# Causal mask added by TensorE: a matmul with the identity, one minimum over both groups, exponential from PSUM

## The chip, the core and the metric

The kernel runs on one core of a Trainium2 chip (trn2). The metric is the device time of one execution in microseconds (us).

## What is computed

One inference step of a two-layer decoder for a prompt of 512 tokens and 8 short sample sequences. Layer 0 is retention with spatial gating, layer 1 is native sparse attention (NSA), and each has a gated MLP behind it. The change touches only the prompt's share of the attention in layer 1. There are 16 query heads in 4 groups of 4, with a head width of 64, and three branches, each with its own keys and values:

```python
# compressed: 31 blocks of keys, masked by block end, softmax, times v
# selected (br 0) and window (br 1), with SEQ = 512: WINDOW = 512, and SEL_TOPK = 16 >= 8 blocks,
# so both are plain causal attention over all keys
s = jnp.einsum('bqgrd,bkgd->bqgrk', q, k).astype(jnp.float32) * ATTN_SCALE
s = jnp.where(mask, s, NEG)
p = jax.nn.softmax(s, axis=-1)
o = jnp.einsum('bqgrk,bkgd->bqgrd', p, v)
...
o = gates[0] * o_c + gates[1] * o_s + gates[2] * o_w
```

## The kernel before

Each engine has one program, written in its own block, and its instructions run in the order in which they stand there. Semaphores join the engines; `order(ins, sem)` counts a semaphore up when the instruction is done.

The stage runs over 72 units. `attention_unit(n)` splits n into a pair of groups j (0 or 1), a query tile qt of 128 queries (0 to 3), and w from 0 to 8. With w = 0 it is the compressed branch for all four heads of both groups; with w > 0 it is one head r and one branch br, for both groups of the pair at once. A unit with w > 0 has keys = (qt + 1) * 128 keys, that is one to four key tiles, so nine units in a row (a "group" of units) have the same length, and the lengths one to four come twice.

For a unit with w > 0 the work is:

- PE, `scores(n)`: one fp32 matmul per group g2 into its own half of `gemm[n % 2]`, two PSUM banks. The contraction is over 64 rows.
- DVE, `mask(n)`: for each g2 one `tensor_tensor_reduce`: scores times -SCALE plus a causal mask, into SBUF `pr[:, n % 4]`, with the minimum over the keys in `negmax`. The mask tile `causal` has 128 x 512 numbers, zero or 1e30 with a negative sign, of which the last `keys` columns are read.
- ACT, `exps(n)`: for each g2 the exponential in place in `pr`, with scale -1, bias `negmax` and the row sum in `rsum`.
- DVE, `normalise(n)`, one unit later: the reciprocal of the sums. POOL: `pr` times reciprocal times gate.
- PE, `turn_probs(n)`, three units later (LAG = 3): transposes of `pr` into `misc`, one per key tile and g2. Then ACT (n even) or DVE (n odd), `take_probs(n)`: copy of `misc` into `pT`.
- PE, `mix_values(n)`, four units later: `pT` times v into the accumulator of the group; after its nine units ACT and DVE take the heads into hH and hL.

The order on PE is scores(n), turn_probs(n - 3), mix_values(n - 4). On DVE it is mask(n), normalise(n - 1), take_probs(n - 3); on ACT exps(n), take_probs(n - 3). The queries and keys themselves are transposed on PE before and at the start of the stage (`turn_in`) and copied to `qTs`, `ksT`, `kwT` by ACT and DVE in turn (`take_in`). `scores(n)` reuses the bank pair of unit n - 2. The masks are loaded on POOL's queue under the semaphore `b_in`.

The helper `activate` records every ACT instruction at line 1142, and `turn` every transpose at line 552. The scores are lines 973 and 978, the products with v 1003 and 1009, the masks 1777 to 1786.

Of the kernel before, what the change touches and what calls it, by code (L numbers as in the profile page):

```python
# [33 lines left out]
ALU = mybir.AluOpType  # L34
ACT = mybir.ActivationFunctionType
AX_X = mybir.AxisListType.X

P = 128
D = 1024
DC = D // P  # L40
SEQ, DB, DS = 512, 8, 4
# [8 lines left out]
G, R, HD = 4, 4, 64  # L50
# [9 lines left out]
SCALE = HD ** -0.5  # L60
NEG = -1e30
BIG = 3e38
# [11 lines left out]
def shape_constants():  # L74

    pos = np.concatenate([np.tile(PAST + np.arange(DS), DB), np.arange(SEQ)]).astype(np.float64)
    ang = THETA_E[:, None] * pos[None, :]
    c = {}
    c["cos_even"] = np.concatenate([np.cos(ang), np.cos(ang)], 0)
    c["sin_even"] = np.concatenate([-np.sin(ang), np.sin(ang)], 0)  # L80
    co, so = np.zeros((P, NT, 8)), np.zeros((P, NT, 8))
    for t in range(NT):
        a = pos[tile_start(t):tile_start(t) + P, None] * THETA_O[None, :]
        co[:, t], so[:, t] = np.cos(a), np.sin(a)
    c["cos_odd"], c["sin_odd"] = co.reshape(P, -1), so.reshape(P, -1)
    i = np.arange(P)
    diff = i[None, :] - i[:, None]
    dm = np.zeros((P, RH, P))
    for h in range(RH):
        dm[:, h] = np.where(diff >= 0, GAMMA[h] ** np.maximum(diff, 0), 0)  # L90
    c["decay"] = dm.reshape(P, -1)
    s = np.arange(NS)
    ds = np.zeros((NS, RH, NS))
    same = (s[:, None] // DS) == (s[None, :] // DS)
    for h in range(RH):
        d = (s % DS)[None, :] - (s % DS)[:, None]
        ds[:, h] = np.where(same & (d >= 0), GAMMA[h] ** np.maximum(d, 0), 0)
    c["decay_s"] = ds.reshape(NS, -1)
    c["qdecay"] = np.stack([GAMMA[h] ** (i + 1.0) for h in range(RH)]).reshape(1, -1)
    c["qdecay_s"] = np.stack([GAMMA[h] ** (s % DS + 1.0) for h in range(RH)]).reshape(1, -1)  # L100
    c["kdecay"] = np.concatenate([np.stack([GAMMA[h] ** (P - 1.0 - i) for h in range(RH)], 1),
                                  np.stack([GAMMA[h] ** (DS - 1.0 - i % DS) for h in range(RH)], 1)], 1)
    c["tril_t"] = (diff >= 0).astype(np.float64)
    c["same_s"] = same.astype(np.float64)
    c["row_of_s"] = (np.arange(DS)[:, None] == (s % DS)[None, :]).astype(np.float64)
    c["batch_of"] = (s[:, None] // DS == np.arange(DB)[None, :]).astype(np.float64)
    c["ident"] = np.eye(P)
    sel = np.zeros((P, 4, P))
    for q in range(4):
        sel[32 * q, q] = 1  # L110
    c["spread"] = sel.reshape(P, -1)
    x = np.arange(SEQ)
    c["causal"] = np.where(x[None, :] - (SEQ - P) <= i[:, None], 0, NEG)
    cm, cv = np.zeros((P, 4, NCP)), np.zeros((P, 4, NCP))
    for t in range(4):
        ok = (np.arange(NCP) * 16 + 31)[None, :] <= (P * t + i)[:, None]
        cm[:, t], cv[:, t] = np.where(ok, 0, NEG), ok
    c["cmp_mask"], c["cmp_valid"] = cm.reshape(P, -1), cv.reshape(P, -1)
    n = i % 4
    new = np.full((P, DB, DB, DS), NEG)  # L120
    for b in range(DB):
        new[:, b, b, :] = np.where(np.arange(DS)[None, :] <= n[:, None], 0, NEG)
    c["mask_new"] = new.reshape(P, -1)
    pj = np.zeros((P, 2, NCS))
    for j in range(2):
        pj[:, j] = ((i // 64) == j)[:, None]
    c["pair_of"] = pj.reshape(P, -1)
    return {k: np.ascontiguousarray(v, dtype=np.float32) for k, v in c.items()}
# [51 lines left out]
def build_program(nc, a, o):  # L180
    with ExitStack() as ctx:
# [9 lines left out]
        def sb(name, shape, dt=F32, at=None):  # L191
            size = int(np.prod(shape[1:])) * 4
            size = (size + 31) // 32 * 32
            off = place["at"] if at is None else at
            assert off + size <= nc.sbuf_usable_end, (name, off, size)
            t = nc.alloc_sbuf_tensor_at(name, shape, dt, offset=off)
            if at is None:
                place["at"] = off + size
            return t
# [92 lines left out]
        place["at"] = O1  # L292
        qT1, ksT, kwT = sb("qT1", [P, R, SEQ]), sb("ksT", [P, 2, SEQ]), sb("kwT", [P, 2, SEQ])
        pr = sb("pr", [P, 4, 2, SEQ])
        causal = sb("causal_sb", [P, SEQ])
        cmask, cvalid = sb("cmask", [P, 4, NCP]), sb("cvalid", [P, 4, NCP])
        cmx, crs = sb("cmx", [P, 2, R]), sb("crs", [P, 3, 2, R])
        negmax, rsum, rscale = sb("negmax", [P, 4, 2]), sb("rsum", [P, 4, 2]), sb("rscale", [P, 4, 2])
# [133 lines left out]

        def masks_done(n):

            grp, w = n // 9, n % 9
            return 17 * grp + (2 * w + 1)

        def exps_done(n):

            grp, w = n // 9, n % 9  # L440
            return 16 * grp + 2 * w
# [106 lines left out]
        def _(pe):  # L548
# [410 lines left out]
            meet(pe, order, 3)  # L959


            def scores(n):

                j, qt, w, r, br = attention_unit(n)
                slot = gemm[n % 2]
                if n >= 2:
                    pe.wait_ge(masked, masks_done(n - 2))
                rows = slice(qt * P, (qt + 1) * P)
                if w == 0:
                    for r in range(R):  # L970
                        for g2 in range(2):
                            half = slice(64 * g2, 64 * g2 + 64)
                            ins = pe.matmul(slot[:, g2, r * NCP:(r + 1) * NCP], qTs[j][half, r, rows], kcP[half, j, :], start=True, stop=True)
                else:
                    keys = (qt + 1) * P
                    for g2 in range(2):
                        half = slice(64 * g2, 64 * g2 + 64)
                        ins = pe.matmul(slot[:, g2, 0:keys], qTs[j][half, r, rows], (ksT, kwT)[br][half, j, 0:keys], start=True, stop=True)  # L978
                order(ins, s_done)

            def turn_probs(n):
# [156 lines left out]
        def _(act):  # L1138
            order = Order(act, act_c)

            def activate(out, in_, func, sem_=None, **kw):
                order(act.activation(out, in_, func, **kw), sem_)  # L1142
# [229 lines left out]
            def exps(n):  # L1372
                _, qt, w, _, _ = attention_unit(n)
                if w == 0:
                    act.wait_ge(c_sub, n // 9 + 1)
                    part = pr[:, n % 4, :, 0:R * NCP]
                    activate(part, part, ACT.Exp, c_exped, scale=SCALE)
                    return
                keys = (qt + 1) * P
                for g2 in range(2):  # L1380
                    act.wait_ge(masked, masks_done(n) + g2 - 1)
                    part = pr[:, n % 4, g2, 0:keys]
                    activate(part, part, ACT.Exp, exped, bias=negmax[:, n % 4, g2:g2 + 1], scale=-1.0, accum_out=rsum[:, n % 4, g2:g2 + 1])

            def take_probs(n):

# [14 lines left out]
            def take_in(n):  # L1401
                j, z = TURNS[n]
                act.wait_ge(qk_turned, n + 1)
                activate(qTs[j][:, z, :] if z < R else (ksT, kwT)[z - R][:, j, :], misc[:, 2 + n % 2 if n < 6 else 3, :], ACT.Copy, qk_ev[0])

            act.wait_ge(gemm_done, FIRST_CHUNK[O_OUT])
            for n in range(0, 6, 2):
# [68 lines left out]
        def _(dve):  # L1476
# [293 lines left out]
            def mask(n):  # L1770
                _, qt, w, _, _ = attention_unit(n)
                dve.wait_ge(s_done, n + 1)
                if n >= 4:
                    dve.wait_ge(p_turned, n - 3)
                if w == 0:
                    part = pr[:, n % 4, :, 0:R * NCP].rearrange("p g (r m) -> p g r m", r=R)
                    order(dve.tensor_tensor(part, gemm[n % 2][:, :, 0:R * NCP].rearrange("p g (r m) -> p g r m", r=R),
                                            cmask[:, qt, :].unsqueeze(1).unsqueeze(1).to_broadcast([P, 2, R, NCP]), ALU.add), masked)
                    order.wait()
                    order(dve.tensor_reduce(cmx[:, :, :], part, AX_X, ALU.max))  # L1780
                    order.wait()
                    order(dve.tensor_tensor(part, part, cmx[:, :, :].unsqueeze(3).to_broadcast([P, 2, R, NCP]), ALU.subtract), c_sub)
                    return
                keys = (qt + 1) * P
                for g2 in range(2):
                    order(dve.tensor_tensor_reduce(pr[:, n % 4, g2, 0:keys], gemm[n % 2][:, g2, 0:keys], causal[:, SEQ - keys:SEQ], -SCALE, BIG,  # L1786
                                                   ALU.add, ALU.min, negmax[:, n % 4, g2:g2 + 1]), masked)

            def normalise(n):
                j, qt, w, _, _ = attention_unit(n)  # L1790
# [32 lines left out]
            def take_in(n):  # L1823
                j, z = TURNS[n]
                dve.wait_ge(qk_turned, n + 1)
                order(dve.tensor_copy(qTs[j][:, z, :] if z < R else (ksT, kwT)[z - R][:, j, :], misc[:, 2 + n % 2 if n < 6 else 3, :]), qk_ev[1])

            dve.wait_ge(gemm_done, FIRST_CHUNK[O_OUT])
            for n in range(1, 6, 2):
# [290 lines left out]
```

## Time and profile before

| | |
|---|---|
| median of 3 runs | 1784.45 us (1780.91 to 1794.52) |
| profiled execution | 1779.98 us |
| its span, first to last instruction | 1778.3 us |
| mean granted TensorE clock | 0.952 |
| PE, DVE, ACT, POOL busy | 1645.2, 780.4, 687.7, 228.7 us |
| attention stage of the prompt | about 1001 to 1187 us of the span |

All rows below come from the profiled execution. Busy times of PE are of pipelined matmuls, whose ends are modelled, so the distance from one start to the next says more than a single duration. A wait is put down to the engine that came last by the profile.

### The profile page before, as it was taken

The numbers are of one execution on the slowest core, as the hardware profiler recorded it, in microseconds if no ns is written. First come the engines' busy times: TensorE is split into PE (matmuls) and PEld (weight loads), VectorE is DVE, ScalarE is ACT, GpSimd is POOL, SyncE is SP. The second block draws the span as 40 slices with busy tenths as digits, with TensorE's granted clock in tenths as the row PEclk, the third lists the DMA queues.
The fourth block names the chain that finished last, engine by engine and source line by source line (L and its number), as shares of the span: only waits on it lengthen the run. The fifth ranks groups of instructions, "written<-read, shape, count | busy, mean of one in ns | idle before, by whom it ended". The sixth has DMA issues, their size and how long they took to land.

```text
span 1778.3 us, 31022 instructions
## 1 busy us (share of the span) xinstructions
PE 1645.2 (93%) x12943; PEld 1508.0 (85%) x12943; DVE 780.4 (44%) x1243; ACT 687.7 (39%) x1303; POOL 228.7 (13%) x586
## 2 busy tenths in 40 slices
PE   4899997999999999978899899989978999999996
PEld 2889987889999999967899655567868999999995
DVE  2544544345542455343211466652135553155523
ACT  4122123445542455223222365654235553255522
POOL 2000001200010000002011344432100000000000
PEclk8899999999999999987999899998788999999998
DMA  6122226403233322324433210013211223332231
GB/s 204 48 74 71 82 91 129 120 25 91 75 87 96 96 71 80 88 86 93 176 101 66 45 43 1 1 31 113 58 48 48 81 77 90 101 92 73 73 86 50
DMA packets 189974, 140.56 MB, mean 79 GB/s; under 512 B 15504, under 2 KB 181664, under 8 KB 189808
## 3 DMA queue, kind: packets, MB, share of 16 engines
q1 hardware_dynamic: 179632, 107.36, 21.5%
q0 software_dynamic: 10240, 31.80, 6.3%
q8 instruction: 69, 1.13, 0.3%
q14 instruction: 33, 0.27, 0.0%
HBM read 130.32 MB, written 13.01 MB: 81 GB/s over the span
## 4 chain that ended last, share of the span: by engine, by line
PE 81%; DVE 7%; ACT 4%; DMA 3%; issue 2%; POOL 1%; POOLq 1%; SPq 0%; DVEq 0%; ACTq 0%
PE gemm L843 39%; PE gemm L577 16%; PE gemm L593 8%; PE misc L552 5%; PE gemm L1114 2%; PE gemm L978 1%; PE misc L1009 1%; DMA raw<-in_o_w_in 1%; ACT pr L1142 1%; DVE pr L1786 1%; DVE hL L1495 1%; DVE y L1512 1%; DVE y L1502 1%; PE misc L613 1%; PE misc L931 1%
## 5 line engine op out<-in xcount | busy, mean ns | idle before, releaser
L1484 DVE TENSOR_TENSOR wL<-raw,wH 128x2048 fp32r<-128x2048 f32 (+2 forms) x107 | 222.1, 2076 | 260.2 <-ACT wH L1142 260.1
L843 PE MATMUL gemm<-hH,wH 128*128 128x272 f32 x1280 | 268.4, 291 | 0.0
L843 PE MATMUL gemm<-hH,wL 128*128 128x272 f32 x1280 | 264.8, 288 | 0.0
L843 PE MATMUL gemm<-hL,wH 128*128 128x272 f32 x1280 | 264.0, 288 | 0.0
L1142 ACT ACTIVATE wH<-raw 128x2048 fp32r<-128x2048 f32 (+2 forms) x107 | 185.3, 1732 | 55.5 <-PE gemm L577 31.1
L843 PEld LDWEIGHTS gemm<-hH,wH 128*128 128x128 f32 x1280 | 200.5, 188 | 5.9 <-issue 5.0
L843 PEld LDWEIGHTS gemm<-hL,wH 128*128 128x128 f32 x1280 | 201.1, 188 | 0.0
L843 PEld LDWEIGHTS gemm<-hH,wL 128*128 128x128 f32 x1280 | 199.9, 189 | 0.0
L593 PE MATMUL gemm<-wH,hH 128*128 128x256 f32 x560 | 166.3, 297 | 23.4 <-ACT vN L1142 10.5
L1706 DVE SCALAR_TENSOR_TENSOR conv<-up,rows_t,conv 128x560 f32<-128x560 f32 x88 | 70.6, 802 | 218.4 <-ACT conv L1142 218.4
L593 PE MATMUL gemm<-wL,hH 128*128 128x256 f32 x560 | 163.8, 292 | 0.0
L593 PE MATMUL gemm<-wH,hL 128*128 128x256 f32 x560 | 162.6, 290 | 0.0
L577 PE MATMUL gemm<-hH,wH 128*128 128x272 f32 (+1 forms) x656 | 142.0, 298 | 7.7 <-DVE hL L1495 4.1
L577 PE MATMUL gemm<-hL,wH 128*128 128x272 f32 (+1 forms) x656 | 137.9, 292 | 0.0
L577 PE MATMUL gemm<-hH,wL 128*128 128x272 f32 (+1 forms) x656 | 137.9, 292 | 0.0
L593 PEld LDWEIGHTS gemm<-wH,hH 128*128 128x128 f32 x560 | 110.9, 198 | 28.4 <-ACT vN L1142 10.7
L1142 ACT ACTIVATE up<-gemm 128x32 f32<-128x32 f32 (+2 forms) x264 | 66.0, 324 | 175.9 <-PE gemm L843 154.4
L577 PEld LDWEIGHTS gemm<-hH,wH 128*128 128x128 f32 (+1 forms) x656 | 105.1, 192 | 13.7 <-issue 8.6
L593 PEld LDWEIGHTS gemm<-wH,hL 128*128 128x128 f32 x560 | 111.8, 200 | 0.0
L593 PEld LDWEIGHTS gemm<-wL,hH 128*128 128x128 f32 x560 | 111.2, 199 | 0.0
L843 PE MATMUL gemm<-aH,wH 128*128 128x272 f32 x528 | 110.1, 290 | 0.0
L843 PE MATMUL gemm<-aH,wL 128*128 128x272 f32 x528 | 108.9, 287 | 0.0
(329 smaller groups left out, 2765.2 us busy)
## 6 DMA issues: line engine op xcount, KB each, us to landing
raw<-in_f_w_in SPq DMA_DIRECT2D x88, 512.0 KB, 5.0
raw<-in_f_w_out SPq DMA_DIRECT2D x32, 704.0 KB, 4.6
raw<-in_e_w_in SPq DMA_DIRECT2D x12, 1024.0 KB, 5.1
raw<-in_o_w_in SPq DMA_DIRECT2D x10, 1024.0 KB, 5.3
raw<-in_e_w_out SPq DMA_DIRECT2D x4, 1024.0 KB, 6.8
pages<-in_cache_cmp POOLq DMA_DIRECT2D x16, 256.0 KB, 5.1
raw<-in_o_w_out SPq DMA_DIRECT2D x16, 256.0 KB, 5.9
rows<-in_cache_sel POOLq DMA_DIRECT2D x12, 256.0 KB, 3.0
```

The lines of the kernel that those rows point to most:

```text
L552: ins = pe.transpose(out, in_, ident[base:base + k, base:base + k])
L577: ins = pe.matmul(gemm[c % 2][0:m, n, 0:TH], w, x[:, k, n * TH:(n + 1) * TH], start=(n_k == 0 and part == 0), stop=(n_k == nk - 1 and part ...
L593: ins = pe.matmul(gemm[c % 2][:, 0, 0:width], x, w, start=(k == 0 and part == 0), stop=(k == DC - 1 and part == 2))
L613: ins = pe.matmul(misc[:, 1 + q // 2, (q % 2) * TQ:(q % 2 + 1) * TQ], spread[:, q, :], rr[:, :], start=True, stop=True)
L843: ins = pe.matmul(gemm[odd][:, n, 0:TH], w, x[:, k, n * TH:(n + 1) * TH], start=(k == 0 and part == 0), stop=(k == nk - 1 and part == 2))
L931: ins = pe.matmul(b7[:, z * 2 * NCP:(z + 1) * 2 * NCP], (phiK2, phiV2)[z][:, l, :], cPT[:, 2 * z:2 * z + 2, l:l + 16 * (NCP - 1) + 1:16], ...
L978: ins = pe.matmul(slot[:, g2, 0:keys], qTs[j][half, r, rows], (ksT, kwT)[br][half, j, 0:keys], start=True, stop=True)
L1009: ins = pe.matmul(misc[64 * g2:64 * g2 + 64, 2 + grp % 2, r * P:(r + 1) * P], kvN[:, 1 + kt, (2 * br + 3) * 256 + g * HD:(2 * br + 3) * 25 ...
L1114: pe.matmul(out, v, pTs[0:k, br, kt, 64 * j:64 * j + 64], start=(br == 0 and kt == 0), stop=False)
L1142: order(act.activation(out, in_, func, **kw), sem_)
L1484: order(dve.tensor_tensor(unit_view(wL, u), unit_view(raw, u), unit_view(wH, u).bitcast(F32), ALU.subtract), lo_ready)
L1706: order(dve.scalar_tensor_tensor(conv[:, j, :], U[:, j, 1:1 + CW], w[:, 17:18], conv[:, j, :], ALU.mult, ALU.add))
```

## The change

The causal tile shrinks to 128 x 128 numbers, zero or plus 1e30. The keys are scaled by -SCALE when they are copied out of PSUM, so the scores arrive negated and scaled. After the two score matmuls PE adds the mask to the last key tile of each group by a matmul of the identity with `causal`. DVE takes one minimum over both groups straight from PSUM and writes nothing but `negmax`. ACT reads the exponential's input straight from PSUM. So the scores of unit n + 2 wait for the exponentials of unit n (for the mask only where n is a w = 0 unit), PE waits for the load of the masks, and ACT has the wait for the free `pr` buffer.

```diff
-    c["causal"] = np.where(x[None, :] - (SEQ - P) <= i[:, None], 0, NEG)
+    c["causal"] = np.where(i[None, :] <= i[:, None], 0, -NEG)
...
-        causal = sb("causal_sb", [P, SEQ])
+        causal = sb("causal_sb", [P, P])
...
         def masks_done(n):
-            grp, w = n // 9, n % 9
-            return 17 * grp + (2 * w + 1)
+            return n + 1
...
+            pe.wait_ge(b_in, BIN_LOADS)
+
             def scores(n):
...
-                if n >= 2:
+                if n >= 2 and (n - 2) % 9 == 0:
                     pe.wait_ge(masked, masks_done(n - 2))
+                elif n >= 2:
+                    pe.wait_ge(exped, exps_done(n - 2))
...
-                        ins = pe.matmul(slot[:, g2, 0:keys], qTs[j][half, r, rows], (ksT, kwT)[br][half, j, 0:keys], start=True, stop=True)
+                        pe.matmul(slot[:, g2, 0:keys], qTs[j][half, r, rows], (ksT, kwT)[br][half, j, 0:keys], start=True, stop=False)
+                    for g2 in range(2):
+                        ins = pe.matmul(slot[:, g2, keys - P:keys], ident[:, :], causal[:, :], start=False, stop=True)
...
                 for g2 in range(2):
-                    act.wait_ge(masked, masks_done(n) + g2 - 1)
+                    if g2 == 0:
+                        act.wait_ge(masked, masks_done(n))
+                        if n >= 4:
+                            act.wait_ge(p_turned, n - 3)
                     part = pr[:, n % 4, g2, 0:keys]
-                    activate(part, part, ACT.Exp, exped, bias=negmax[:, n % 4, g2:g2 + 1], scale=-1.0, accum_out=rsum[:, n % 4, g2:g2 + 1])
+                    activate(part, gemm[n % 2][:, g2, 0:keys], ACT.Exp, exped, bias=negmax[:, n % 4, g2:g2 + 1], scale=-1.0, accum_out=rsum[:, n % 4, g2:g2 + 1])
...
-                activate(qTs[j][:, z, :] if z < R else (ksT, kwT)[z - R][:, j, :], misc[:, 2 + n % 2 if n < 6 else 3, :], ACT.Copy, qk_ev[0])
+                activate(qTs[j][:, z, :] if z < R else (ksT, kwT)[z - R][:, j, :], misc[:, 2 + n % 2 if n < 6 else 3, :], ACT.Copy, qk_ev[0],
+                         scale=1.0 if z < R else -SCALE)
...
-                for g2 in range(2):
-                    order(dve.tensor_tensor_reduce(pr[:, n % 4, g2, 0:keys], gemm[n % 2][:, g2, 0:keys], causal[:, SEQ - keys:SEQ], -SCALE, BIG,
-                                                   ALU.add, ALU.min, negmax[:, n % 4, g2:g2 + 1]), masked)
+                order(dve.tensor_reduce(negmax[:, n % 4, :], gemm[n % 2][:, :, 0:keys], AX_X, ALU.min), masked)
...
-                order(dve.tensor_copy(qTs[j][:, z, :] if z < R else (ksT, kwT)[z - R][:, j, :], misc[:, 2 + n % 2 if n < 6 else 3, :]), qk_ev[1])
+                order(dve.tensor_scalar(qTs[j][:, z, :] if z < R else (ksT, kwT)[z - R][:, j, :], misc[:, 2 + n % 2 if n < 6 else 3, :],
+                                        1.0 if z < R else -SCALE, None, ALU.mult), qk_ev[1])
```

## Rows read from the trace of the kernel before

**Rows 1.** The page, busy time of the engines, us and share of the span.

```profile
PE 1645.2 (93%) x12943; PEld 1508.0 (85%) x12943; DVE 780.4 (44%) x1243; ACT 687.7 (39%) x1303; POOL 228.7 (13%) x586
```

**Rows 2.** Busy time by window (length, then engines), granted clock, DMA share, GB/s.

```profile
1007.00:1012.00 5.00, 4.95 (x26) 3.55 (x24) 1.69 (x10) 2.46 (x7) 1.75 (x4) 0.56 0.00 0
...
sum 186.00, PE 166.78 PEld 105.69 DVE 114.00 ACT 108.37 POOL 81.75; mean PE 16.68 PEld 10.57 DVE 11.40 ACT 10.84 POOL 8.18
```

**Rows 3.** Timeline of PE, two units of three key tiles: start, us, what, idle before.

```profile
1139.42 0.92 PE L978 MATMUL gemm<-ksT,qT 64*128 64x384 f32 x4
1140.27 0.88 PE L552 MATMUL misc<-ident_sb,pr 128*128 128x128 f32 x6
1141.08 0.88 PE L1009 MATMUL misc<-pT_rows,kvN 128*64 128x128 f32 x12
1141.88 0.92 PE L978 MATMUL gemm<-kwT,qT 64*128 64x384 f32 x4
1143.13 0.85 PE L552 MATMUL misc<-ident_sb,pr 128*128 128x128 f32 x6 [0.33 <-ACT pT_rows L1142]
...
1144.71 0.92 PE L978 MATMUL gemm<-ksT,qT 64*128 64x384 f32 x4
```

**Rows 4.** The chain that ended last, the same unit: start, us, what.

```profile
1139.50 0.87 PE gemm L978 x4
1140.39 0.56 DVE pr L1786
1140.99 0.50 ACT pr L1142
1141.51 0.78 ACT pr L1142 x3
1142.30 0.70 ACT pT_rows L1142
```

**Rows 5.** Waits in the stage: who for whom, us in total, times, longest.

```profile
PE misc L552 <- ACT pT_rows L1142: 8.7, 17, 1.3
...
PEld gemm L978 <- DVE negmax L1786: 4.0, 12, 0.8
```

**Rows 6.** The chain elsewhere: a retention product, and scores of four key tiles.

```profile
193.47 0.89 PE misc L661 x8
...
1086.37 1.08 PE gemm L978 x4
```

**Rows 7.** Groups by shape in the stage, DVE's masks and ACT's exponentials: busy, mean ns.

```profile
L1142 ACT ACTIVATE pr<-pr,negmax 128x512 f32<-128x512 f32 x32 | 22.8, 715 | 19.0 <-DVE negmax L1786 19.0
...
L1786 DVE CUSTOM_DVE_ANT_0 pr<-gemm,causal_sb 128x512 f32<-128x512 f32 x32 | 20.8, 687 | 12.2 <-PE gemm L978 12.2
...
L1786 DVE CUSTOM_DVE_ANT_0 pr<-gemm,causal_sb 128x384 f32<-128x384 f32 x32 | 16.6, 556 | 12.0 <-PE gemm L978 11.7
...
L1142 ACT ACTIVATE pr<-pr,negmax 128x128 f32<-128x128 f32 x32 | 12.6, 394 | 10.5 <-DVE negmax L1786 10.4
L1786 DVE CUSTOM_DVE_ANT_0 pr<-gemm,causal_sb 128x256 f32<-128x256 f32 x32 | 12.2, 419 | 5.3 <-PE gemm L978 5.3
...
L1786 DVE CUSTOM_DVE_ANT_0 pr<-gemm,causal_sb 128x128 f32<-128x128 f32 x32 | 8.0, 288 | 10.0 <-PE gemm L978 9.9
```

**Rows 8.** Groups by shape in the whole span, instructions of DVE and ACT that read PSUM.

```profile
L1848 DVE TENSOR_REDUCE csm<-gemm 128x8 f32<-128x120 f32 x1 | 0.3, 283 | 0.3 <-PE gemm L1077 0.3
...
L1814 DVE COPY pT_rows<-misc 128x1024 f32<-128x1024 f32 x8 | 9.7, 1214 | 5.9 <-PE misc L552 5.9
...
L1142 ACT ACTIVATE kT<-gemm,eps 128x544 f32<-128x544 f32 x1 | 0.7, 716 | 0.0
```

**Rows 9.** Timeline of POOL's queue before the stage.

```profile
985.13 0.56 POOL L2042 DMA_DIRECT2D pair_of_sb<-in_pair_of  x1
```

**Rows 10.** Timeline of PE where a one-tile group follows a four-tile one.

```profile
1092.80 0.49 PE L978 MATMUL gemm<-ksT,qT 64*128 64x128 f32 x4
...
1095.28 0.49 PE L978 MATMUL gemm<-kwT,qT 64*128 64x128 f32 x4
```

## The prediction

> **What bounds the kernel now.** I read the page first: TensorE (PE) is busy 93% of the span [rows 1], but that share is a mean over stages. The change sits in one stage, the prompt's attention. The table of windows [rows 2] cuts it out: from 1001 to 1187 us, 186 us in which PE is busy 166.8, VectorE (DVE) 114.0, ScalarE (ACT) 108.4 and GpSimd (POOL) 81.8. No other engine is near full, yet PE is not full either, so the question is what ends its pauses.
>
> PE's own timeline over two units of three key tiles [rows 3] answers it. Scores start at 1139.42 and 1141.88 and again at 1144.71: two units take 5.29 us. PE's work in them is 2 x (0.85 + 0.81 + 0.80) = 4.92 us, start to start; the rest is one pause before a transpose, put down to ACT's copy of the probabilities to pT. The chain of waits [rows 4] spells out the same 5.29 us: scores 0.89 with the step to DVE, first mask 0.60 until ACT starts, the two exponentials with their sums 1.31, ACT's copy 0.83 until PE starts, and then, from [rows 3], 1.58 for transposes and products with V until the next scores, 5.21 in all with 0.08 of rounding and steps. ACT's copy for unit n-3 stands behind the exponentials of unit n in ACT's order, and PE's transpose for n-2 needs misc, so it waits for the copy. DVE copies the other parity with less to do, so this cycle turns once in two units. In the list of waits [rows 5] it is the longest that PE's matmuls have here. So PE's work and the cycle through DVE and ACT lie within 0.4 us of each other, and the change lengthens both.
>
> **The change, part by part.**
>
> Mask matmuls. Each of the 64 units with w > 0 gets two more fp32 matmuls, 128 x 128 weights and 128 moving columns. An fp32 matmul is two instructions in this trace (a unit's two score matmuls are x4 [rows 3]), so four more per unit. The nearest row is the retention product of exactly this shape [rows 6]: eight instructions in 0.89 us, 0.111 each. Hence M = 4 x 0.111 = 0.445 us per unit. Ends of the cost: below, what 128 more columns cost in the 64-row scores, 1.08 us with four key tiles against 0.87 with three [rows 6, 4], 0.053 for each of four instructions, M = 0.21; above, the transposes at 0.81 us for six [rows 3], 0.135 each, M = 0.54. I take 0.445, for the shape is the same. The mask matmuls stand between the scores and s_done, so they lie on both paths.
>
> By the Trainium skill (VectorE: DVE Perf Modes, section on the TRN2 errata) a matmul costs the larger of 60 cycles and 6 plus its columns; an estimate by it is 134 cycles, 0.056 us, for each of the four, so M = 0.22. The row of the same shape has twice that, so here the trace disagrees.
>
> Minimum. Two DVE instructions per unit become one over both groups. Only the first stood between scores and first exponential: 0.288, 0.419, 0.556, 0.687 us for one to four key tiles [rows 7]. The new one must pass over both groups first. A reduce straight from PSUM took 0.283 us for 120 elements and a PSUM copy of 1024 elements 1.214 [rows 8]: 1.03 ns per element behind some 0.16 us. That gives 0.42, 0.69, 0.95, 1.21 us for 256 to 1024 elements, so the exponential starts 0.12, 0.26, 0.39, 0.52 us later (a readout tail of 0.01 taken off). DVE's own total hardly changes, since the second mask and two readouts go.
>
> Exponential from PSUM. Same count, 128 instructions, in this trace from SBUF only: 0.715 us for 512 [rows 7]. The nearest from PSUM, with a bias from memory too, is a square root over 544 at 0.716 [rows 8]; from 128 to 512 elements the exponential grows by 0.84 ns each, so those 32 elements are 0.027, and PSUM saves about 0.025 each, 0.05 in a unit's two. Ends: nothing, and 0.1.
>
> Waits. The scores of unit n+2 now wait until both exponentials of n have read the bank, not only the mask. In the three-tile unit that is 0.87 + 0.445 + 0.98 + 1.31 = 3.6 us after the scores began, and PE comes back to that bank after some 6 us, so it is covered by 2.4 us. What would queue behind it on PE are transposes and products of older units. ACT's new wait for p_turned is for a transpose that PE does before it starts scores n, so it is always over. PE's new wait for b_in costs nothing: its loads stand on POOL's queue before that of pair_of, issued at 985.13 [rows 9], and the stage begins at 1001; if they were late, DVE would wait for them in the kernel before. The smaller causal tile is a smaller one of them. The copies of keys get a constant factor: the same activation on ACT; on DVE a copy becomes a scalar multiply from PSUM, which I cost at nothing, since there are only two such for keys and four for queries, early in the stage. Were each 0.3 us longer with no cover, it would be 2 us. The masked wait that remains after a unit w = 0 is as before.
>
> **Sum.** The cycle turns once for two units, so 32 times with w > 0, 8 for each number of key tiles. It grows by M + reduce - exponential: 0.445 + 0.12 - 0.05 = 0.515, then 0.655, 0.785, 0.915; together 2.87, times 8 = 23.0 us. PE's own work in two three-tile units grows by 0.89 to 5.81, still under the cycle's 5.29 + 0.785 = 6.07. Two additions: where a group of one tile follows one of four, PE is bound outright (scores at 1092.80 and 1095.28, 2.48 apart with eight transposes and sixteen products between, and no pause [rows 10]), so some four units pay M each instead of half a growth, +0.8; and from 1007 to 1012 the granted clock is 0.56 [rows 2], near the lower level of 1.2 GHz, where M doubles for some two units, +1. In all +25 us. The profiled execution took 1779.98 us, its span 1778.3 with 1.7 around it, so it becomes 1805; the median of the runs shown is 4.5 higher: 1784.45 + 25 = 1809.
>
> **Rivals.**
> (a) The mask matmul costs by its columns alone, M = 0.21. The cycle loses 32 x 0.235 = 7.5 us of its growth: +17, 1801. For it: the 64-row scores pay that. Against: the row of the same shape.
> (b) Not slower by 1%: the minimum runs at two elements per cycle. Then over both groups it takes what one takes now, the exponential starts no later, and M less 0.05 is left: 32 x 0.395 + 1.8 = +14, 1799; with (a) as well +7, 1791. It decides from a reduce of 1024 under some 0.85 us. Against it: reduce and copy from PSUM at one element per cycle [rows 8].
> (c) The bank held by the exponentials becomes the wait. Once per group ACT copies the heads, beside its usual copy of probabilities, before the next exponentials; if scores lose 1 us there, eight groups give +8: +33, 1817. It decides if ACT runs over 2.4 us late. For it: the bank now has two more instructions behind it, on another engine. Against: the waits of the scores for a masked bank come to only 4.0 us in the whole stage [rows 5].
>
> **How the numbers follow.** My forecast, +19 to +31, gets 0.68; (a) 0.12; (b) 0.05; (c) 0.12; something else 0.03. A measurement of this kernel tells about 1%, 18 us, from no change. Slower by more than that: the forecast, (c) and part of (a), less a little for the spread of the runs, 0.82. Within 1%: the rest of (a), and (b), 0.15. Faster: 0.03, since no part removes more than 2 us from the cycle. The range runs from (a) less the spread of the runs before, 1796, to just above (c), 1821.
>
> **What would show it.** Right: the mask matmuls are 256 instructions, spaced 0.11 us; the reduce of 1024 takes 1.2 us; the attention stage lasts 186 + 25 us; two three-tile units go from 5.29 to 6.1; outside the stage nothing moves. Wrong: mask instructions spaced near 0.05 (a), a reduce of 1024 near 0.7 (b), scores that wait for ACT's pr for more than a few us in total (c); or a granted clock under 1.0 after 1012 us, which would lengthen a stage this full by its own share.

## The result, and the profile after

The changed kernel takes 1815.85 us in the median of four runs (1814.32 to 1816.18) against 1789.49 of the kernel before (1780.91 to 1800.19, four runs): ratio 1.0143, 95% interval 1.0081 to 1.0205. It is slower by 26.4 us, where 25 were forecast. A second measurement, with five runs of the changed kernel, gave 1.0147 (1.0116 to 1.0178). The profiled execution took 1816.18 us with a span of 1814.5, so beside the 1778.3 of before it is 36 us longer. Eleven of those are not in the part that was changed, and the agreement of the medians has some luck in it; both are taken apart below.

The head of the page after, to be read beside [rows 1]: PE has 256 instructions more, DVE 192 fewer.

```profile
span 1814.5 us, 31403 instructions
...
PE 1691.6 (93%) x13199; PEld 1548.9 (85%) x13199; DVE 776.1 (43%) x1051; ACT 684.4 (38%) x1303; POOL 228.6 (13%) x586
```

The groups by shape after, from just before the attention stage on (busy, mean ns, idle before). They answer to [rows 7, 8]:

```profile
L983 PE MATMUL gemm<-causal_sb,ident_sb 128*128 128x128 f32 x256 | 46.1, 303 | 0.0
...
L1147 ACT ACTIVATE pr<-gemm,negmax 128x512 f32<-128x512 f32 x32 | 21.7, 683 | 28.9 <-DVE negmax L1794 28.9
...
L1794 DVE TENSOR_REDUCE negmax<-gemm 128x2 f32<-128x1024 f32 x16 | 19.6, 1224 | 19.4 <-PE gemm L983 19.4
...
L1794 DVE TENSOR_REDUCE negmax<-gemm 128x2 f32<-128x768 f32 x16 | 15.3, 958 | 21.1 <-PE gemm L983 21.1
...
L1147 ACT ACTIVATE pr<-gemm,negmax 128x128 f32<-128x128 f32 x32 | 11.5, 363 | 16.9 <-DVE negmax L1794 16.7
...
L1794 DVE TENSOR_REDUCE negmax<-gemm 128x2 f32<-128x512 f32 x16 | 11.0, 690 | 11.3 <-PE gemm L983 11.3
...
L1794 DVE TENSOR_REDUCE negmax<-gemm 128x2 f32<-128x256 f32 x16 | 6.8, 424 | 16.3 <-PE gemm L983 16.3
```

The minimum over both groups takes 0.42, 0.69, 0.96 and 1.22 us, the exponential 0.683 and 0.363 where it took 0.715 and 0.394: 0.03 saved by PSUM.

PE's timeline after, two units of three key tiles as in [rows 3] (start, us, what, idle before):

```profile
1159.63 0.92 PE L981 MATMUL gemm<-kwT,qT 64*128 64x384 f32 x4
1160.48 0.71 PE L983 MATMUL gemm<-causal_sb,ident_sb 128*128 128x128 f32 x4
1161.35 0.85 PE L551 MATMUL misc<-ident_sb,pr 128*128 128x128 f32 x6 [0.16 <-ACT pT_rows L1147]
1162.13 0.88 PE L1014 MATMUL misc<-pT_rows,kvN 128*64 128x128 f32 x12
1162.93 0.92 PE L981 MATMUL gemm<-ksT,qT 64*128 64x384 f32 x4
1163.78 0.71 PE L983 MATMUL gemm<-causal_sb,ident_sb 128*128 128x128 f32 x4
1164.33 0.82 PE L551 MATMUL misc<-ident_sb,pr 128*128 128x128 f32 x6
1165.08 0.88 PE L1014 MATMUL misc<-pT_rows,kvN 128*64 128x128 f32 x12
1165.88 0.92 PE L981 MATMUL gemm<-kwT,qT 64*128 64x384 f32 x4
```

Two units take 1165.88 - 1159.63 = 6.25 us, before 5.29. The four mask instructions take 0.55 from their first start to that of the transposes (1163.78 to 1164.33), 0.137 each. The pause before one transpose in two is still there, still put down to ACT's copy to pT, and shorter: 0.16 us where [rows 3] have 0.33. The chain of waits after runs through the same places as [rows 4], with the mask's 0.64 in it:

```profile
1163.01 0.85 PE gemm L981 x4
1163.85 0.64 PE gemm L983 x4
...
1166.00 0.76 ACT pr L1147 x3
1166.76 0.71 ACT pT_rows L1147
...
1167.60 0.85 PE misc L551 x6
```

In the list of waits of the stage, to be read beside [rows 5], the scores' weight loads now wait for the exponentials that hold the bank (us in total, times, longest):

```profile
PEld gemm L981 <- ACT pr L1147: 6.4, 15, 0.8
```

The attention stage, from the first scores to the end of the last product, is 999.0 to 1211.1, 212.1 us, against 1000.5 to 1187.5, 187.0 before: +25.1. The next stage is the attention of the sample group, whose code the change doesn't touch. From the start of its first product to that of its last it takes 1220.4 to 1294.9, 74.5 us, before 1196.9 to 1258.7, 61.8: +12.7. From there to the end of the program both take 519.6 us. The changed kernel came to its first scores 1.5 us sooner, and together this is the 36 us. The windows of after and before over the stretch go with it (length, busy PE, PEld, DVE, ACT, POOL, granted clock, DMA):

```profile
1220.00:1295.00 75.00, 73.94 (x366) 58.51 (x362) 14.52 (x56) 22.09 (x56) 10.28 (x21) 0.67 0.25 77
```

```profile
1197.00:1259.00 62.00, 61.06 (x362) 49.08 (x362) 13.72 (x54) 20.76 (x54) 10.28 (x21) 0.82 0.28 93
```

The same products at a mean granted clock of 0.67 instead of 0.82.

### The profile page after: what moved, and what is told of

Same layout as the page of the kernel before. It is cut to its first block, busy times and chain, and to the rows that moved or that the text cites. A ratio compares the mean times of both kernels' runs of the same rounds, so it can differ in the third digit from the quotient of the medians.

```text
span 1814.5 us, 31403 instructions
## 1 busy us (share of the span) xinstructions
PE 1691.6 (93%) x13199; PEld 1548.9 (85%) x13199; DVE 776.1 (43%) x1051; ACT 684.4 (38%) x1303; POOL 228.6 (13%) x586
## 4 chain that ended last, share of the span: by engine, by line
PE 82%; DVE 6%; ACT 4%; DMA 3%; issue 2%; POOL 1%; POOLq 1%; SPq 0%; ACTq 0%; DVEq 0%
PE gemm L842 38%; PE gemm L576 16%; PE gemm L592 8%; PE misc L551 5%; PE gemm L1119 2%; PE misc L1014 2%; PE gemm L981 2%; PE gemm L983 1%; DMA raw<-in_o_w_in 1%; ACT pr L1147 1%; ACT pT_rows L1147 1%; DVE hL L1504 1%; DVE y L1521 1%; DVE y L1511 1%; PE misc L612 1%
## 5 line engine op out<-in xcount | busy, mean ns | idle before, releaser
L592 PE MATMUL gemm<-wH,hH 128*128 128x256 f32 x560 | 166.2, 297 | 23.2 <-ACT vN L1147 10.5
```

Source lines behind the costliest of these rows:

```text
L592: ins = pe.matmul(gemm[c % 2][:, 0, 0:width], x, w, start=(k == 0 and part == 0), stop=(k == DC - 1 and part == 2))
```

## The experiments

Two readings are used for each. The ratio is of the whole time, against the kernel before on the same chip. And each profile gives the distance between the w = 0 units, nine units of one length; where the granted clock is full, two profiles of one kernel agree in it to 0.1 us, so it tells what the ratios can't. In us; sample products go from the start of the first to that of the last. A star marks a stretch that was partly at half clock; the first group of the stage, where nearly all profiles have some half clock, is left out of that. Two to four tiles are the first group of that length, but for two tiles in "before, copy first", whose first was at half clock:

| kernel | ratio (95%) | 1 tile, after 4 | 2 tiles | 3 tiles | 4 tiles | attention stage | sample products |
|---|---|---|---|---|---|---|---|
| before | | 18.8 | 18.6 | 23.2 | 27.9 | 187.0 | 61.8 |
| changed | 1.0143 (1.0081 to 1.0205) | 22.4 | 21.1 | 27.4 | 31.7 | 212.1 | 74.5 |
| before + mask matmuls | 1.0115 (1.0076 to 1.0155) | 21.7 | 20.7 | 25.9 | 30.5 | 206.2 | 75.6 |
| changed - mask matmuls | 1.0044 (1.0008 to 1.0081) | 20.0* | 19.1 | 24.7 | 29.1 | 198.2* | 74.3 |
| changed, two minima | 1.0104 (1.0064 to 1.0144) | 21.5 | 20.6 | 25.6 | 30.5 | 206.2 | 74.4 |
| before, bank held | 1.0004 (0.9956 to 1.0052) | 20.4* | 18.6 | 23.2 | 27.9 | 192.5* | 74.5 |
| changed, mask in fp32r | 1.0152 (1.0122 to 1.0182) | 21.1 | 20.0 | 26.2 | 30.4 | 205.0 | 74.4 |
| before, copy first | 1.0020 (0.9979 to 1.0061) | 17.3 | 18.1 | 21.3 | 28.0 | 190.3* | 75.9 |
| changed, copy first | 1.0139 (1.0109 to 1.0169) | 20.8 | 20.3 | 25.1 | 30.4 | 204.1 | 75.5 |

**The mask matmuls alone, in the kernel before.**

```diff
-                        ins = pe.matmul(slot[:, g2, 0:keys], qTs[j][half, r, rows], ..., start=True, stop=True)
+                        pe.matmul(slot[:, g2, 0:keys], qTs[j][half, r, rows], ..., start=True, stop=False)
+                    for g2 in range(2):
+                        ins = pe.matmul(slot[:, g2, keys - P:keys], ident[:, :], causal[:, SEQ - P:SEQ], start=False, stop=True)
```

(PE also waits for the load of the masks, once, ahead of the stage.)

> The kernel before with the two mask matmuls of each unit added and nothing else changed (DVE still adds the mask and takes one minimum per group). The attention stage lasts 187 us before and 212 after. Theory (the matmuls lie on PE's path and on the cycle scores, DVE, ACT's copy, transposes): M was measured at 0.55 us, so 32 x 0.55 and a few units that pay in full, +18 to +22: stage 205 to 209. Rival (they hide in PE's pauses and the later exponential is the whole loss): stage 187 to 194. On the stage behind it (sample attention: 61 us before, 73 after, at a lower granted clock): if a fuller PE ahead of it brings the clock down earlier, it lasts over 70 here; if that is chance or phase, it may lie anywhere from 55 to 75.

The stage grows by 19.2 us, to 206.2, as expected. With three tiles two units go from 5.29 to 5.93 us, and there PE has no pause left: its work is 2 x (0.85 + 0.55 + 0.75 + 0.80) = 5.90. The matmuls are most of the growth, and they don't hide.

**The change without them.**

```diff
-                    for g2 in range(2):
-                        ins = pe.matmul(slot[:, g2, keys - P:keys], ident[:, :], causal[:, :], start=False, stop=True)
```

The score matmuls then end their own accumulation, and the kernel leaves the causal mask out.

> The changed kernel without the mask matmuls; it leaves the causal mask out. Theory: the stage loses 18 to 22 us of 212, to 190 to 194, so that the minimum over both groups is left with +10 less 2 for the exponential from PSUM. Rival (the held bank is the wait, not the matmuls): it loses under 10 us and the scores still wait for ACT's exponentials as long as now (6.4 us in total).

The stage took 198.2 us, more than the 190 to 194 expected, with half clock from about 1109 to 1123, in the second one-tile group and the two-tile group behind it. That two-tile group took 22.1 us where the first one took 19.1, so 3 of the 4 us above the expected come from there. At full clock two, three and four tiles cost 0.5, 1.5 and 1.2 us over the kernel before for nine units. PE's timeline of three tiles here:

```profile
1149.69 0.92 PE L981 MATMUL gemm<-kwT,qT 64*128 64x384 f32 x4
1151.27 0.84 PE L551 MATMUL misc<-ident_sb,pr 128*128 128x128 f32 x6 [0.66 <-ACT pT_rows L1145]
1152.05 0.88 PE L1012 MATMUL misc<-pT_rows,kvN 128*64 128x128 f32 x12
1152.85 0.92 PE L981 MATMUL gemm<-ksT,qT 64*128 64x384 f32 x4
...
1155.31 0.92 PE L981 MATMUL gemm<-kwT,qT 64*128 64x384 f32 x4
```

5.62 us for two units, 0.33 over before, where the prediction had 0.39 - 0.05 = 0.34. The pause before the transpose has grown from 0.33 to 0.66, by what the later exponential alone would give. With the matmuls it is 6.25, so on this cycle they cost 0.63 together; the first two experiments add up to the change in each group to 0.2 us: for two tiles 2.1 + 0.5 against 2.5, for three 2.7 + 1.5 against 4.2, for four 2.6 + 1.2 against 3.8. The scores wait for ACT's exponentials as long as in the change, 6.9 us against 6.4; that wait didn't go with the matmuls. Whether it costs anything is taken up further down, with the held bank.

**Two minima again.**

```diff
-                order(dve.tensor_reduce(negmax[:, n % 4, :], gemm[n % 2][:, :, 0:keys], AX_X, ALU.min), masked)
+                for g2 in range(2):
+                    order(dve.tensor_reduce(negmax[:, n % 4, g2:g2 + 1], gemm[n % 2][:, g2, 0:keys], AX_X, ALU.min), masked)
```

(with ACT waiting for each minimum in turn and the count of minima as before)

> The changed kernel with one minimum for each group again, so that the first exponential starts when the first group's minimum is there. Theory: the exponential starts 0.12 to 0.52 us earlier and the cycle gives that back, 10 us, until PE's own work ends it (three tiles: cycle 6.25 us, PE's work 6.04): 6 to 10 us, stage 202 to 206. Rival (the exponential's start is covered, PE is the bound everywhere): 0 to 2 us.

The stage is 5.9 us shorter than the changed kernel's, just under the 6 to 10 expected, but its first group took 2.6 us more (21.8 against 19.2), at half clock from 1002 to 1011, where the changed kernel had it full from about 1004 on. The other seven groups gain 8.4: 0.5, 1.8 and 1.2 for two, three and four tiles, 0.9 for one, and in the second half much the same. Three tiles are at PE's own 5.90 us. So the one minimum for both groups costs what the kernel with the mask matmuls still had above PE's work, and no more than that can be had back.

**The bank held, in the kernel before.**

```diff
-                if n >= 2:
+                if n >= 2 and (n - 2) % 9 == 0:
                     pe.wait_ge(masked, masks_done(n - 2))
+                elif n >= 2:
+                    pe.wait_ge(exped, exps_done(n - 2))
```

> The kernel before, with scores n + 2 waiting for the exponentials of n as in the change, although the bank is free after the masks. Theory: covered by some 2 us, stage 187 to 188, whole time unchanged within 2 us. Rival (c): +1 us for each of eight groups, stage 194 to 196.

The ratio is 1.0004, and the groups with full clock take 18.6, 23.2 and 27.9 us, the same as before to the tenth. Yet the profile reports more waits of the scores than before:

```profile
  ACT pr L1144: 8.9, 23
  issue: 7.3, 35
  DVE negmax L1788: 1.0, 5
```

8.9 us in 23 pauses, where the kernel before had 4.0 in 12 for the mask, and nothing lost. They are pauses of the weight loads; that PE would otherwise have paused a little later, at the transpose, is the likely reading, not one that was tested. Rival (c) falls. In the changed kernel the exponentials come later, so there the bank is held longer; but the growth of the two experiments above, of which only the second holds the bank, adds up to the whole to 0.2 us a group and leaves no room for it there either. The stage as a whole took 192.5 us where 187 to 188 were expected, 5.1 us of the difference in the two groups that have half clock in this stretch:

```profile
1106.00:1124.00 18.00, 16.95 (x88) 9.54 (x88) 8.40 (x43) 8.03 (x33) 7.19 (x15) 0.53 0.01 1
```

**The mask in one pass.** Identity and mask tile are copied once into fp32r tiles.

```diff
+            order(dve.tensor_copy(causal_r[:, :], causal[:, :]), mask_r)
+            order(dve.tensor_copy(ident_r[:, :], ident[:, :]), mask_r)
...
-                        ins = pe.matmul(slot[:, g2, keys - P:keys], ident[:, :], causal[:, :], start=False, stop=True)
+                        ins = pe.matmul(slot[:, g2, keys - P:keys], ident_r[:, :], causal_r[:, :], start=False, stop=True)
```

> The changed kernel with the mask matmul in fp32r (identity and mask tile copied once into fp32r tiles by DVE), so one instruction for each group in place of two. Theory: M falls from 0.55 to about 0.28 us, on the cycle 32 x 0.27, the attention stage from 213 to 203 to 206 us at full clock; nine units of three tiles from 27.35 to about 26.2, of two tiles from 21.1 to 20. Rival (a fixed cost of switching to the identity dominates, not the two passes): under 3 us.

As expected: 26.2 us for three tiles and 20.0 for two, the stage at 205.0. The two instructions left take 0.27 us:

```profile
1153.18 0.44 PE L985 MATMUL gemm<-causal_r,ident_r 128*128 128x128 f32 x2
1153.45 0.84 PE L553 MATMUL misc<-ident_sb,pr 128*128 128x128 f32 x6
```

0.135 us for each, as for those in fp32, so the gain comes from half the number of instructions. The whole time is no better than the changed kernel's (1809.9 us against 1808.57 on the same chip). Their profiles differ by 7.1 us in the attention stage, and the stage behind it moves either by more than that, as is shown further down.

**ACT's copy ahead of its exponentials,** in the kernel before and in the changed one. This tests the cycle itself.

```diff
-                if n < N_UNITS:
-                    exps(n)
-                if 1 <= n < 7 and n % 2:
-                    take_in(5 + n)
                 if LAG <= n < N_UNITS + LAG:
                     take_probs(n - LAG)
+                if n < N_UNITS:
+                    exps(n)
+                if 1 <= n < 7 and n % 2:
+                    take_in(5 + n)
```

> The kernel before with ACT's copy of the probabilities of unit n - 3 put ahead of the exponentials of unit n. It tests the cycle on which the prediction rests. Theory: the cycle is cut and PE's own work or DVE's copy is left: for three tiles 5.29 us for two units become 4.95 to 5.1, nine units 23.2 become 21.8 to 22.5, the attention stage 6 to 11 us shorter. Rival (the copy's place does not matter, because PE waits for POOL's scaling): within 1 us, or longer, since the exponentials start later.

> The same reordering in the changed kernel. Theory: nine units of three tiles from 27.35 us to about 26.2 (PE's own work with M at 0.55 is 6.04 for two units against 6.25), the stage 5 to 10 us shorter; the sooner copy also takes the later exponential off the path, so the growth over the kernel before, reordered too, is only the mask matmuls: 64 x 0.55 less the switch that the transposes save. Rival: the exponentials, now later still, hold the bank, and the scores wait for them by more than the 6.4 us of now.

In the kernel before, reordered, PE has no pause in three tiles:

```profile
1143.48 0.92 PE L978 MATMUL gemm<-kwT,qT 64*128 64x384 f32 x4
1144.33 0.87 PE L552 MATMUL misc<-ident_sb,pr 128*128 128x128 f32 x6
1145.13 0.88 PE L1009 MATMUL misc<-pT_rows,kvN 128*64 128x128 f32 x12
1145.93 0.92 PE L978 MATMUL gemm<-ksT,qT 64*128 64x384 f32 x4
...
1148.39 0.92 PE L978 MATMUL gemm<-kwT,qT 64*128 64x384 f32 x4
```

4.91 us for two units, PE's own work; nine units 21.3. In the whole stage the transposes wait for ACT's copy 0.4 us instead of 8.7. The wait of their weight loads for POOL's scaling, the longest that PE has in the kernel before (34.6 us in total), stays at 29.6, so it isn't what ended the pauses. Four tiles gain nothing (28.0). In the changed kernel it is 5.90 us (nine units 25.1), and two, three and four tiles differ between the two reordered kernels by 2.2, 3.8 and 2.4 us. For three tiles that is 8 x 0.475, the matmuls and nothing for the minimum. So the cycle through ACT's copy is what the kernel before waits for with up to three tiles, and the changed one with four as well (30.4 against 31.7); the later exponential hurts only through it. The stage of the reordered kernel before was not 6 to 11 us shorter, as expected, but 3.3 longer, and the whole isn't faster (1.0020). In its profile the clock stayed at half until 1033, where the kernel before had it full from about 1011 on, and the first two groups took 26.1 and 21.4 us against 19.2 and 18.6. The changed kernel, reordered, has its stage 8.0 us shorter, within the 5 to 10 expected.

**Both kernels once more,** to see how much of a profile belongs to its kernel.

> The changed kernel once more, on the chip of the other runs of this call. Theory: the attention stage is again 212 to 214 us if its clock is full; the sample stage behind it, with products over 74.5 us at a mean granted clock of 0.67 in the first profile, is not bound to this kernel: the runs spread over 15 us or more as those of the kernel before do (1770 to 1801). Rival: the change pulls the clock down there every time, all runs within 2 us of each other near 1815.

> The kernel before once more. Its first profile had the clock full for 30 us of the sample stage (products over 61.8 us, mean granted clock 0.82). Theory: the clock there is chance, not a property of either kernel: this profile has the attention stage at 187 to 189 us where its clock is full, and the sample products anywhere between 57 and 76 us. Rival (the kernel before keeps the clock, the changed one loses it): 60 to 63 us again, and runs within 4 us of 1784.

| profile | attention stage | sample products | granted clock in them | span |
|---|---|---|---|---|
| before | 187.0 | 61.8 | 0.82 | 1778.3 |
| before again | 188.9 | 66.5 | 0.76 | 1782.9 |
| changed | 212.1 | 74.5 | 0.67 | 1814.5 |
| changed again | 212.1 | 57.0 | 0.90 | 1792.2 |

The two profiles of the changed kernel are 22.3 us apart, and their attention stages agree to a tenth of a us. Of the difference 17.5 us lie in the sample products and 5.0 ahead of the attention stage (it starts at 999.0 and 994.0). The window of the second, to be read beside that of the first above:

```profile
1215.00:1273.00 58.00, 56.86 (x366) 45.91 (x362) 14.10 (x56) 20.99 (x57) 10.37 (x21) 0.90 0.33 100
```

The times of the kernel before, 85 runs on three chips beside these experiments, spread from 1770.35 to 1801.13 us (median 1788.34), the five of the changed one in its second measurement from 1793.92 to 1815.17. The first profile of before, 1779.98 us, lies below the median of its kind, and the first of the changed kernel, 1816.18, above every run of its second measurement.

**A probe of the clock in the sample stage.** Matmuls of the identity with itself, into columns that nobody reads, are added to the kernel before: eight in a block ahead of each batch's products, or eight spread, two behind each three products. The kernel with the spread ones also has ACT's copy ahead of its exponentials, as above. The edit of the spread ones:

```diff
                             pe.matmul(out, v, pTs[0:k, br, kt, 64 * j:64 * j + 64], start=(br == 0 and kt == 0), stop=False)
+                        for _ in range(2):
+                            pe.matmul(misc[:, 3, 3 * P:4 * P], ident[:, :], ident[:, :], start=True, stop=True)
```

> The kernel before with eight matmuls of the identity with itself (128 x 128, fp32) in one block ahead of the products of each sample batch, into a part of a bank that nobody reads; a probe of the clock in that stage. At full clock a batch takes 7.0 us and the block 8 x 0.22 = 1.8. Theory (the clock falls there because PE's work is thin): it stays up more, and the products take 57 to 72 us in spite of 14 us of filler. Rival (the clock there has nothing to do with how full PE is, or the block is in the wrong place): 74.5 + 20, 90 us or more.

> The same number of fillers spread, two after the three products of each branch and half, and in the attention stage the copy of the probabilities ahead of the exponentials as in the reordered kernel before. Theory: attention 180 to 182 us at full clock (nine units of three tiles 21.3 us); the clock in the sample stage full through most of it, products 60 to 68 us, whole time 1775 to 1785. Rival: the fillers cost more than the clock returns, 1795 or more.

In a block (ratio 1.0031, 0.9998 to 1.0064) the products take 78.1 us at a mean clock of 0.82: less than the rival's 90, more than the 57 to 72 of the theory. Spread (1.0018, 0.9983 to 1.0054), the clock is full up to 1262:

```profile
1202.00:1217.00 15.00, 15.00 (x104) 12.57 (x104) 3.54 (x14) 4.13 (x12) 4.04 (x8) 1.00 0.48 151
1217.00:1262.00 45.00, 45.00 (x315) 36.40 (x315) 10.14 (x40) 15.41 (x40) 6.20 (x13) 1.00 0.24 78
1262.00:1281.00 19.00, 15.53 (x80) 13.22 (x81) 1.70 (x5) 3.85 (x7) 1.27 (x3) 0.71 0.00 1
```

and the ten runs spread over 6 us only, 1790.4 to 1796.27, where those of the kernel before beside them went from 1771.46 to 1800.18. But the products take 74.7 us, not 60 to 68, and the whole 1792.04 in the median, not 1775 to 1785: the filler costs what the clock returns. The attention stage was not the 180 to 182 us expected but 190.0, again with half clock in the reordered start, from 1016 to 1038.

**The version that should have beaten both:** the reordering from unit 18 on only, and half of the spread fillers.

```diff
+                if 18 <= n < N_UNITS + LAG:
+                    take_probs(n - LAG)
                 if n < N_UNITS:
                     exps(n)
...
-                if LAG <= n < N_UNITS + LAG:
+                if LAG <= n < 18:
                     take_probs(n - LAG)
```

> A version that may beat both: the kernel before, with ACT's copy ahead of the exponentials only from unit 18 on (the reordering from the start had half clock from 1016 to 1036 in both profiles, 7 us), and with half the spread fillers in the sample stage, one after the products of each branch and half. Theory: attention 181 to 183 us; the sample products 60 to 67 us, at full clock but for their end, and less scattered than now; whole time 1773 to 1780, against a median of 1788 or so of the kernel before. Rival: half the fillers don't hold the clock and the products take 75 to 80 us: 1790 or more.

The attention stage is 181.0 us, as expected, 6 less than before. The clock of the sample stage isn't held by half the fillers, as the rival said (two of its windows):

```profile
1220.00:1240.00 20.00, 20.00 (x115) 15.61 (x115) 4.14 (x16) 6.38 (x16) 4.30 (x9) 0.83 0.31 99
1240.00:1260.00 20.00, 20.00 (x115) 15.52 (x115) 4.06 (x16) 6.39 (x16) 0.00 (x0) 0.83 0.05 19
```

79.1 us of products where 60 to 67 were hoped for, 1788.7 us in the median where 1773 to 1780 were, ratio 1.0028 (0.9999 to 1.0058): no gain. The late reordering without fillers was not tried.

## Why the prediction was right

The bound. PE's work and the cycle scores, DVE, ACT's exponentials, ACT's copy, transposes lie close together: shown for three tiles, by 5.29 us turning into 4.91 when only the copy's place changed. The prediction read the cycle there and took it over to all four lengths. With four tiles it doesn't hold: in the first such group of the kernel before the transposes wait 0.3 us for ACT's copy and 1.0 for DVE's, and the reordering gains nothing. The mask matmuls alone leave no such pause in that group, so they cost there what they add to PE's own work less the pauses, 8 x 0.49 - 1.3 = 2.6 us, as measured. That the cycle's sum for four tiles, 3.7, came close to the measured 3.8 is luck.

Mask matmuls. Right in place, short in size. The step that took M from the row of the same shape, "M = 4 x 0.111 = 0.445", was mis-sized: the four take 0.55 us from start to start, add 0.49 to PE's own work (the transposes behind them shrink by 0.06), and 0.63 to the cycle. The upper end of 0.54, taken from the transposes, was nearer. Rival (a), the column price, is refuted with 0.137 an instruction: an estimate by the rule of the Trainium skill (VectorE: DVE Perf Modes, section on the TRN2 errata) had 0.056.

Minimum. Right to 0.01 us an instruction and in what it costs: 0.33 of 0.34 us in the three-tile cycle, nothing where PE is the bound. Rival (b) needed a reduce of 1024 under 0.85 us; it takes 1.224.

Exponential. 0.03 us saved in each, 0.025 forecast; ACT's read of the row sum behind each takes 0.196 us for 0.187, so 0.02 is left.

Held bank. Covered, as forecast: with it alone no group at full clock moved by a tenth. The prediction's own sign of rival (c), scores that wait for ACT's pr for more than a few us in total, did appear, with 6.4 us, and it misled: the list of waits gives the held bank 6 to 9 us that cost nothing. Whether a wait costs is decided by the cycle around it, not by its sum.

Sum. 25.1 us in the attention stage for 25, with errors that cancel. By groups of nine units the growth was 0, 2.5, 4.2, 3.8, 3.6, 2.6, 4.1 and 4.4 with the end, where the cycle's sum had 2.1, 2.6, 3.1, 3.7 and again. For three tiles the forecast was 1.0 short, 4 x 0.18 = 0.7 of it by the size of M. The first group grew by nothing: the allowance of +1 for half clock went the other way, and the changed kernel had the clock full from about 1004 instead of 1011. That the matmuls brought this about is not shown: the kernel before with the mask matmuls had half clock from about 1006 to 1010 in its profile, and the changed one with two minima up to 1011.

Outside the stage. "Nothing moves" failed for the profile, by some 11 us, and held for the code: the sample stage has no set time, in either kernel. The forecast of 1805 for the profiled execution, against 1816.18, is off by that. The 1809 for the median is 7 us off 1815.85, and 5 of these are the fourth run of the kernel before, which moved its median from 1784.45 to 1789.49.

## What to carry to other kernels

Work moved from a slack engine to the full one must be priced twice, in the full engine's own work and in the cycle that it closes, and the path that is longer afterwards counts: with three tiles the mask matmuls cost PE's own work 0.98 us in two units and the cycle 0.63, and both then stood at 5.9. A merged reduction that halves DVE's instructions delays the first consumer by its second half. Price a short matmul among others of another shape by its neighbours in the stage, not by a run of its own kind. And before one blames a change for a stage that it didn't touch, take a second profile of both kernels: here the same program gave 57.0 and 74.5 us for the same products.

## What the runs showed of the hardware

- TensorE's granted clock can lie near its lower level in a stage in which PE is busy by the profile. In the sample stage of the changed kernel PE is busy 73.9 of 75 us, with short matmuls of 64 columns, and is granted 0.67 on the mean, and from 1226 on between 0.50 and 0.78 in every window of 6 us. In the same kernel it was 0.90 in another execution. With two 128 x 128 x 128 matmuls of the identity behind every three products it was 1.00 for 60 us in the one profile taken, and the ten runs lay within 6 us. Why one execution keeps the clock and the next doesn't stays open.
- In the attention stage, behind its first 16 us, it fell to half only in kernels without the mask matmuls: for 17 us from the second one-tile group on in the kernel with the held bank, for 14 there in the changed kernel without the matmuls, for some 7 in the second profile of the kernel before, and until 1033 and 1038 in the two kernels reordered from the start. In none of the five kernels with the mask matmuls did it fall between 1016 and the end of that stage. Nor did it in the first profile of the kernel before, so the matmuls are not shown to be the reason.
- A matmul of 128 x 128 weights and 128 columns takes 0.135 us in fp32r and 0.137 per instruction in fp32 between scores and transposes, but 0.111 in a run of its own kind [rows 6]. The products with V, with the same 128 columns and 64 columns of weights, take 0.80 / 12 = 0.067 [rows 3], so the moving columns alone don't set the price. Where these differences come from was not tried.
